# Four more first-use places for expert 0's weights, router logits in four column groups, and transposes by token chunk

## What is computed

```python
def expert_choice_ffn(h, w_router, w_gate, w_up, w_down):
    B, S, D = h.shape                              # 1, 512, 1024
    cap = EC_CAPACITY_FACTOR * S // N_EXPERTS      # 2 * 512 // 16 = 64
    logits = jnp.einsum('bsd,de->bse', h.astype(jnp.float32), w_router.astype(jnp.float32))
    affinity = jax.nn.softmax(logits, axis=-1)
    top_w, top_idx = lax.top_k(affinity.transpose(0, 2, 1), cap)
    xe = jax.vmap(lambda hb, ib: hb[ib])(h, top_idx)
    hid = jax.nn.silu(jnp.einsum('becd,edf->becf', xe, w_gate)) * jnp.einsum('becd,edf->becf', xe, w_up)
    ye = jnp.einsum('becf,efd->becd', hid, w_down) * top_w[..., None].astype(h.dtype)
    combine = lambda yb, ib: jnp.zeros((S, D), h.dtype).at[ib.reshape(-1)].add(yb.reshape(-1, D))
    return jax.vmap(combine)(ye, top_idx)
...
        x = x + gate1 * token_mixer(h, ...)
        h = rms_norm(x, norm_ffn_w[l]) * (1.0 + scale2) + shift2
        x = x + gate2 * expert_choice_ffn(h, ...)
```

## Time and profile before

| | |
|---|---|
| median of three runs | 2085.09 us |
| the profiled execution, its own time | 2085.79 us |
| its span (first to last instruction) | 2084.0 us |
| TensorE busy, matmuls | 1924.8 us, 92% |
| VectorE busy | 684.4 us, 33% |
| ScalarE busy | 463.1 us, 22% |
| DMA bytes | 513.42 MB, mean 246 GB/s |

### The profile page before, as it was taken

The page is one execution under the profiler, slowest core; times in us unless marked ns, Lnnn a source line. Parts: engine busy times, 40 slices in busy tenths (PEclk is TensorE's granted clock), DMA queues, the critical chain, the costliest instruction groups (busy, mean ns, idle before and its releaser), DMA issues.

```text
span 2084.0 us, 20330 instructions
## 1 busy us (share of the span) xinstructions
PE 1924.8 (92%) x8674; PEld 1156.3 (55%) x8674; DVE 684.4 (33%) x943; ACT 463.1 (22%) x685; POOL 32.7 (2%) x41
## 2 busy tenths in 40 slices
PE   5999979999879999889999999898999999999998
PEld 5876766567544434343433434343344478888887
DVE  5474464375321111211110021101038842322334
ACT  5347445212201001010100001010031422222222
POOL 0000000000000000000000000000030000000000
PEclk9999989999989999999999999999999999999999
DMA  7211110484649999999999999999971105323211
GB/s 300 84 51 48 61 41 21 178 300 188 262 195 421 421 421 421 422 421 421 421 422 421 421 421 421 421 421 421 392 234 41 41 23 169 91 91 101 101 61 41
DMA packets 131775, 513.42 MB, mean 246 GB/s; under 512 B 8035, under 2 KB 70627, under 8 KB 81379
## 3 DMA queue, kind: packets, MB, share of 16 engines
q1 hardware_dynamic: 127312, 487.95, 59.2%
q10 hardware_dynamic: 4374, 24.18, 3.0%
HBM read 510.00 MB, written 2.10 MB: 246 GB/s over the span
## 4 chain that ended last, share of the span: by engine, by line
PE 69%; DMA 19%; DVE 7%; ACT 3%; issue 2%; POOL 0%; SPq 0%; ACTq 0%; DVEq 0%; POOLq 0%
DMA work<-in_w_exp_up 11%; PE ps L1119 11%; PE ps L1080 7%; DMA ring<-in_w_exp_up 6%; PE ps L1284 5%; PE ps L534 5%; PE ps L1244 4%; PE ps L1243 4%; PE ps L1245 4%; PE ps L550 3%; PE ps L1007 3%; PE ps L551 3%; PE ps L552 3%; PE ps L733 2%; PE ps L1105 2%
## 5 line engine op out<-in xcount | busy, mean ns | idle before, releaser
L1080 PE MATMUL ps<-work 128*64 128x512 f32 x1208 | 328.8, 594 | 25.7 <-DMA work<-in_w_exp_up 25.7
L1080 PE MATMUL ps<-ring,work 128*64 128x512 f32 x720 | 216.8, 594 | 15.0 <-DMA ring<-in_w_exp_up 15.0
L1080 PEld LDWEIGHTS ps<-work 128*64 128x64 f32 x1208 | 112.0, 137 | 201.2 <-issue 149.5
L2206 DVE TENSOR_TENSOR work<-work,ps 64x512 f32<-64x512 f32 x64 | 42.0, 691 | 477.4 <-ACT work L1650 476.7
L1650 ACT ACTIVATE work<-ps 64x512 f32<-64x512 f32 x64 | 32.6, 584 | 734.4 <-PE ps L1080 734.4
L534 PE MATMUL ps<-work,ring 128*128 128x512 f32 x320 | 138.9, 592 | 0.7 <-issue 0.7
L1119 PE MATMUL ps<-work 128*64 128x512 f32 x568 | 135.1, 628 | 4.2 <-issue 3.6
L1243 PE MATMUL ps<-xh,wh 128*128 128x512 f32 x352 | 137.0, 389 | 0.0
L1245 PE MATMUL ps<-xh,wl 128*128 128x512 f32 x352 | 136.9, 389 | 0.0
L1244 PE MATMUL ps<-xl,wh 128*128 128x512 f32 x352 | 136.9, 389 | 0.0
L2339 DVE TENSOR_TENSOR wl<-ring,wh 128x2048 fp32r<-128x2048 f32 x33 | 75.6, 2292 | 180.2 <-ACT wh L1738 180.2
(11 more groups left out here) (337 smaller groups left out, 2604.4 us busy)
## 6 DMA issues: line engine op xcount, KB each, us to landing
work<-in_w_exp_gate SPq DMA_DIRECT2D x76, 1024.0 KB, 26.7
work<-in_w_exp_up SPq DMA_DIRECT2D x75, 1024.0 KB, 27.3
work<-in_w_exp_down SPq DMA_DIRECT2D x71, 1024.0 KB, 27.0
ring<-in_w_exp_gate SPq DMA_DIRECT2D x45, 1024.0 KB, 26.7
ring<-in_w_exp_up SPq DMA_DIRECT2D x45, 1024.0 KB, 27.0
ring<-in_w_exp_down SPq DMA_DIRECT2D x42, 1024.0 KB, 26.8
ring<-in_w_in SPq DMA_DIRECT2D x27, 1024.0 KB, 6.4
work<-in_ada_w ACTq DMA_DIRECT2D x16, 1024.0 KB, 6.6
```

Source lines behind the costliest of these rows:

```text
L1080: i = e.matmul(PS[64 * gu:64 * gu + 64, fb, :], at(XET + 128 * k + 64 * z, 64), flat(key)[:, 512 * fb:512 * fb + 512], start=(k == 0), sto ...
```

## The change

- **Places.** Four are added: 19, 20 and 21 lie over `YE`, the residual `X` and the first part of `HIDT` (hidden values, transposed), 22 over `SG` (silu's output; until the logits are done the same space holds the first half of `H2T`). `HIDT` and `XET` change their order for it. Each is used once, by expert 0: 21 and 22 by its last gate and up piece (`eg`, `eu` of `k` = 7), 19 and 20 by its 4th and 5th down piece. The first three open when the last chunk of `XS2` is written, the fourth when the logits are done. From the 22nd expert piece on, the cycle of 17 goes on as before, four pieces later.
- **Residual.** Since `X` is overwritten, the first pair's results are added to `XS2` times the root mean square instead (`st2 + 4`), and the sum is written to `X`. For this the reciprocals go to `st2`.
- **Transposes.** All 8 `k` of a token chunk are transposed as soon as the chunk is in `XS2`, each `k` into a bank of its own (`T2_BANKS`).
- **Logits.** They stand behind all transposes; slice `k` goes to the rows from 32 (k mod 4) of bank 2, so that four partial sums arise. DVE copies 128 x 512 instead of 16 x 512, and the turn to tokens x experts is a product with a 128 x 16 matrix of ones and zeros (built by one new small DVE reduction) that also adds the four groups.
- **Gather.** For the first pair, `k` 0 to 4 stand ahead of expert 0's first gate and up slice, `k` 5 to 7 between its first and its second.
- Some semaphores are merged (`ap_vc` into `ap_va`, `a_lb` into `a_c`, `mu_pe` and `vr_pe` into `ln_pe`, `l_gf` into `l_vec`), with the same order.

The core of the diff:

```diff
-SLOT = [HEAD + W * i for i in range(NR0)] + [SG + W * (i + 1) for i in range(3)] + [HT, HT + W] + [HIDT + 1024 + W * i for i in range(5)] + [DEAD]
+SLOT = [HEAD + W * i for i in range(NR0)] + [SG + W * (i + 1) for i in range(3)] + [HT, HT + W] + [XET + 1024 + W * i for i in range(5)] + [DEAD]
 SLOT += [HGT, PT + 3072]
+SLOT += [YE, YE + W, YE + 2 * W, SG]
...
     cycle = (12, 13, 14, 15, 8, 16, 2, 4, 7, 11, 9, 10, 1, 5, 3, 0, 6)
-    slots += [cycle[i % 17] for i in range(len(ex))]
+    slots += list(cycle[:14]) + [21, 22] + list(cycle[14:]) + [19, 20] + [cycle[(i - 4) % 17] for i in range(21, len(ex))]
...
-                    elif slot == 6:
+                    elif slot in (6, 22):
                         e.wait_ge(s["wo_pe"], 8)
                         e.wait_ge(s["rt_pe"], 1)
+                    elif slot in (19, 20, 21):
+
+                        e.wait_ge(*normed(2, 3))
...
                 e.wait_ge(*turned_k(2, k))
-                if k == 0:
-                    e.wait_ge(s["wo_t"], 5)
-                return e.matmul(PS[0:16, 4, :], at(O_VEC + VEC["wr"][0] + 16 * k, 16), at(H2T + 512 * k, 512), start=(k == 0), stop=(k == KD - 1))
+                g = 32 * (k % 4)
+                return e.matmul(PS[g:g + 16, 2, :], at(O_VEC + VEC["wr"][0] + 16 * k, 16), at(H2T + 512 * k, 512), start=(k < 4), stop=(k >= 4))
...
-            turn(XS2, [0, 1, 2, 3], lambda c: normed(2, c), t2_free, s["t_pe"], lambda k: logits(k - 2) if k >= 2 else None)
-            logits(KD - 2)
-            logits(KD - 1).then_inc(s["rt_pe"], 1)
+            for c in range(TC):
+                e.wait_ge(*normed(2, c))
+                for k in range(KD):
+                    if c == 0:
+                        t2_free(k)
+                    i = e.transpose(bank(T2_BANKS[k], 128, 128 * c), at(XS2 + 1024 * c + 128 * k, 128), ident)
+                    if c == TC - 1:
+                        i.then_inc(s["t_pe"], 1)
+            for k in range(KD):
+                i = logits(k)
+            i.then_inc(s["rt_pe"], 1)
+
+            def logits_by_token():
+                for tc in range(TC):
+                    p = e.matmul(bank(5, 16, 16 * tc), at(WKT + 128 * tc, 128), at(rst, 16), start=True, stop=True)
+                p.then_inc(s["rt_pe"], 1)
...
-            gather(0)
+            gather(0, range(5))
             for ex in range(NE):
                 z, p = ex % 2, ex // 2
                 for k in range(KD):
 
+                    if (ex, k) == (0, 1):
+                        gather(0, range(5, KD))
...
+            own(e.tensor_reduce(at(rst, 16), raw(O_CST + CST["ident"][0], [(1, 16), (32, 4)]), AX, ALU.add))
             e.wait_ge(s["rt_pe"], 1)
             e.wait_ge(*rooted(2, 3))
-            e.tensor_copy(rows(0, 16, WKT, 512), PS[0:16, 4, :]).then_inc(s["rt_d"], 1)
+            e.tensor_copy(at(WKT, 512), bank(2)).then_inc(s["rt_d"], 1)
...
+                if p == 0:
+
+                    e.scalar_tensor_tensor(out=xa, in0=at(XS2 + 1024 * tc + 512 * dh, 512), scalar=at(st2 + 4 + tc, 1), in1=bank(6 + dh),
+                                           op0=ALU.mult, op1=ALU.add).then_inc(s["x_ca"], 1)
+                    return
                 e.tensor_tensor(xa, xa, bank(6 + dh), ALU.add).then_inc(s["x_ca"], 1)
```

More of the change, by code:

```diff
@@ L72 @@
 XS2, H2T = PT, HT + 4096
-AFFT, WKT = X + 4096, X + 4608
+AFFT, WKT = X + 5120, X + 5632
 SG = HT + 4096
 YE = X - 1024
-XET, HIDT = X + 4096, X + 5120
+HIDT, XET = X + 4096, X + 5120
 OH, OHW, OHWT = GATE1, GATE1 + 512, O_SMALL + NSMALL - 512
@@ L175 @@
 SEMS = (
-    "l_vec l_cst l_x l_ab l_gf l_out "
-    "own_act own_dve p_zero a_c d_small a_lb d_ada "
+    "l_vec l_cst l_x l_ab l_out "
+    "own_act own_dve p_zero a_c d_small d_ada "
     "r_a r_d sc1 t_pe t_d t_a ac_pe "
@@ L361, in rooms_of @@
             return piece(key, 4 if kind in ("wo", "o2") else 8)
+        T2_BANKS = (2, 3, 4, 5, 6, 7, 0, 1)
         FS_O2, FS0 = 4, 8
@@ L617, in hg_proj @@
                     if g < 2 and pr == 1:
-                        e.wait_ge(*((s["ap_w"], 5), (s["ap_va"], 1))[g])
+                        e.wait_ge(*((s["ap_w"], 5), (s["ap_va"], 2))[g])
                     elif g in (2, 3):
@@ L694, in at_proj @@
                 norm_rot(4)
-                e.wait_ge(s["ap_vc"], 1)
+                e.wait_ge(s["ap_va"], 1)
                 for tc in range(TC):
@@ L822, in values @@
                     if u == 0:
-                        e.wait_ge(s["ap_va"], 1)
+                        e.wait_ge(s["ap_va"], 2)
                     e.wait_ge(s["at_c"], 2 * u + 2)
@@ L974, in _ @@
             e.wait_ge(s["rt_d"], 1)
-            e.wait_ge(s["wo_t"], 6)
-            by_token()
+            logits_by_token()
             e.wait_ge(s["rt_d"], 3)
@@ L994, in hidden, with gather @@
                 return rows(64, 128, SG + 512 * fb + 256 * (q // 2), 256).rearrange("p (i a) -> p i a", a=2)[:, :, q % 2]
-            def gather(p):
-                e.wait_ge(s["x_oh"], p + 1)
-                for k in range(KD):
+            def gather(p, ks=range(KD)):
+                if ks[0] == 0:
+                    e.wait_ge(s["x_oh"], p + 1)
+                for k in ks:
                     if k == 0 and p > 0:
@@ L1070, in _ @@
                     for fb in range(4):
[L1071 to L1075, removed]
+                        if k == 0 and ex > 0:
+                            e.wait_ge(s["x_hd"], 4 * ex - 3 + fb)
                         for gu, kind in ((0, "eg"), (1, "eu")):
@@ L1188, in _ @@
                 p = e.matmul(bank(4), cst("o512"), at(CV + 512 * i, 512), start=(i == 3), stop=(i == 1))
-            p.then_inc(s["mu_pe"], 1)
+            p.then_inc(s["ln_pe"], 1)
             pool_dense(10, 1, 4)
@@ L1196, in _ @@
                 p = e.matmul(bank(5), cst("o512"), at(TP + 512 * i, 512), start=(i == 0), stop=(i == 3))
-            p.then_inc(s["vr_pe"], 1)
+            p.then_inc(s["ln_pe"], 1)
             pool_dense(13, 0, 4)
@@ L1314, in _ @@
             e.wait_ge(s["d_small"], 1)
-            e.activation(at(lbs, 8), at(lbe, 8), ACT.Exp).then_inc(s["a_lb"], 1)
+            e.activation(at(lbs, 8), at(lbe, 8), ACT.Exp).then_inc(s["a_c"], 1)
             def rms(x, scr, st, chunks, ready, done):
@@ L1336, in turned @@
                         ready()
-                    put(k, bank(banks[k % 4])).then_inc(s["t_a"], 1)
+                    put(k, bank(banks[k % len(banks)])).then_inc(s["t_a"], 1)
             def half_hi(n):
@@ L1424, in at_proj @@
                 e.wait_ge(s["ap_q"], 4)
-                e.activation(at(TMP + 1024, 512), bank(1), ACT.Copy).then_inc(s["ap_vc"], 1)
+                e.activation(at(TMP + 1024, 512), bank(1), ACT.Copy).then_inc(s["ap_va"], 1)
                 for n in ahead(half_no[("at", 2), 1]):
@@ L1712, in _ @@
             pool_out(12, 2)
-            e.wait_ge(s["vr_pe"], 1)
+            e.wait_ge(s["ln_pe"], 2)
             e.wait_ge(s["cv_pe"], 1)
@@ L1833, in _ @@
                 ada_step(k, ACC)
-            e.wait_ge(s["a_lb"], 1)
+            e.wait_ge(s["a_c"], 2)
             own(e.reciprocal(at(lbr, 8), at(lbs, 8)))
@@ L1840, in rms @@
             def rms(i, x, xs, st, chunks, ready):
+                inv = st if i == 2 else st + 4
                 for c in chunks:
                     e.wait_ge(*rooted(i, c))
-                    own(e.reciprocal(at(st + 4 + c, 1), at(st + 4 + c, 1)))
+                    own(e.reciprocal(at(inv + c, 1), at(st + 4 + c, 1)))
                     ready(c)
-                    e.tensor_scalar(at(xs + 1024 * c, 1024), at(x + 1024 * c, 1024), at(st + 4 + c, 1), None, ALU.mult).then_inc(s["r_d"], 1)
+                    e.tensor_scalar(at(xs + 1024 * c, 1024), at(x + 1024 * c, 1024), at(inv + c, 1), None, ALU.mult).then_inc(s["r_d"], 1)
             e.wait_ge(*rooted(1, 3))
@@ L1870, in turned @@
                     e.wait_ge(*turns(i, k))
-                    put(k, bank(banks[k % 4])).then_inc(s["t_d"], 1)
+                    put(k, bank(banks[k % len(banks)])).then_inc(s["t_d"], 1)
             for k in range(KD):
@@ L2320, in _ @@
             pool_window(2)
-            e.wait_ge(s["mu_pe"], 1)
+            e.wait_ge(s["ln_pe"], 1)
             e.wait_ge(s["cv_d"], 93)
@@ L2396, in fin_scale @@
                 if tc == 0:
-                    e.wait_ge(s["l_gf"], 16)
+                    e.wait_ge(s["l_vec"], 32)
                 e.wait_ge(s["fin_x"], 2 * tc + 2)
```

16 lines of the change are left out of this document (9 added, 7 removed).

## The result

The changed kernel takes 2067.49 us (median of four runs, 2067.22 to 2070.18) against 2085.74 for the kernel before in the same series (four runs): 0.9918 of the time, 95% interval 0.9906 to 0.9931, 18.25 us less. Two further series gave 17.1 and 16.3 us less (0.9915 and 0.9921). The forecast was 2065.5, with a range of 2061.5 to 2070.5, and 19.6 us less. So the time lies in the range, and the gain was forecast 1 to 3 us too large.

The account below looks back on a forecast made before the run. The prediction took an unbroken stream of expert weight loads to bound the kernel; -10.0 (places) - 10.8 (earlier release) + 1.2 (hole) = -19.6 us gave a median of 2065.5 us, range 2061.5 to 2070.5.

Parts of the forecast that it names:

- The bound: Expert stage: its end is the end of an unbroken load stream at 421 GB/s; all behind follows at fixed distance.
- The four places, -10.0: Early expert loads: four more pieces fit into idle DMA time before the stream restarts, 2.49 us each, -10.0 us.
- Logits, -8.3: Router: transposes per chunk and side-by-side logits let DVE's logits copy start at 557.4 instead of 565.71, -8.3 us.
- Turn to tokens, +0.3: Router, behind the logits: four products with 128 x 128 weights instead of 16 x 128 cost +0.3 us.
- Gather, -2.8: First pair's gather: 24 records moved behind expert 0's first gate and up slice, so that slice starts 2.8 us earlier.
- the release: First two reused places, after expert 0's first gate and up slice: freed at 588.7 instead of 599.5, -10.8 us.
- The hole of +1.2: Stream's restart: next two releases come 6.2 us later, two pieces fill only 4.98, so DMA idles, +1.2 us.
- The 18th piece, 0.6 us to spare: Stream in expert 0's down: piece waits for the sixth down piece at 631.6, needed at 632.2; no loss.
- the second rival: Reuse distance binds: PE late in expert 0, pieces 15 to 20 wait, total 2068 to 2075.5 us; chance 0.08.
- The groups overlap: Against the rival that the logits' column groups run one after another: +4.2 us, total 2069.7; chance 0.12.
- The places are filled in time: Against the rival that the extra places fill too late, nothing new in place at restart: 2075.5 us; chance 0.04.
- The clock rose within the gather as before: Against the rival that the clock stays at 1.2 GHz through expert 0's gate and up: +26, 2092 us; chance 0.02.

Follow-up runs that it names:

- The late doubled gather: Changed kernel with the gather products of the pair of experts 8 and 9 made twice: 2068.25 us, distance to last `eu` landing 934.5 us.

## Why the prediction was right, and where it was off

**The bound.** Right. The end of the expert stage moves with the last `eu` piece (18.5 us) and nothing behind it changes (583.8 and 583.9 us). The late doubled gather costs nothing, at a busy share that looks like a bound.

**The four places, -10.0.** Right: alone -9.9 by the median, and by the distance once the shorter gather is taken out of its -10.4. The two of them that were taken out cost 4.2 us of distance, 5.0 less the 0.8 of the hole that went with them. They are filled by about 576 (forecast 578) and the stream restarts at 590.

**Logits, -8.3.** The copy comes 8.63 us earlier, counted from the last addition. The copies out of PSUM ran four in a row on both engines, a little faster than by the pair that I had (0.74 instead of 0.83 each):

```profile
551.89 2.97 DVE L2161 TENSOR_SCALAR work<-ps,stay 128x512 f32<-128x512 f32 x4 [0.52 <-PE ps L978]
```

```profile
551.90 2.79 ACT L1654 ACTIVATE work<-ps,stay 128x512 f32<-128x512 f32 x4 [1.52 <-PE ps L978]
```

**Turn to tokens, +0.3.** Mis-sized: 1.08 instead of 0.43, +0.65, since the products come as two records each (x8 against x4). That the copy came 0.3 earlier than forecast makes up for this miss, by luck. And I had taken all behind as unchanged, while the next transposes (L999) took 1.04 us at a granted clock of 0.50, before 0.60 us at 1.00. Up to the gather's start the distance shrank by 7.5 us, not 8.0.

**Gather, -2.8.** The 40 records took 7.16 us, of which I had expected 6.8; the first product of expert 0 came 10.0 us earlier from the last addition, not 10.8, and with it the release (41.05 against 51.06). As a term of the sum it is -2.5.

**The hole of +1.2.** Right, 1.2 (291 GB/s in the window). The prediction's 27.67/8 is 3.46, not 3.43, which moves nothing.

**The 18th piece, 0.6 us to spare.** This step failed. I had divided expert 0's down, 15.65 us, evenly by eight. The clock falls at its start, before and after. The trace of the kernel before had it already: its down began at 628.08, and SP issues on the first piece's release 3.32 us later, not 1.96.

```profile
631.40 0.33 SPq L524 DMA_DIRECT2D work<-in_w_exp_up  x1
```

The changed kernel's windows of PE (us, busy, PEclk, DMA share, GB/s):

```profile
618.00:620.00 2.00, 1.50 (x11) 1.00 1.01 422
620.00:622.00 2.00, 1.94 (x6) 0.60 1.01 422
622.00:624.00 2.00, 2.00 (x8) 0.55 1.02 418
624.00:626.00 2.00, 2.00 (x12) 1.00 0.99 406
```

So the first down piece takes about 3.4 us (SP issues on its release at 623.49, the down began at 620.06), the others 1.7 to 1.95, and the first six take 12.2 instead of 11.7:

```profile
623.49 0.33 SPq L530 DMA_DIRECT2D ring<-in_w_exp_up  x1
625.44 0.33 SPq L530 DMA_DIRECT2D ring<-in_w_exp_gate  x1
627.16 0.33 SPq L530 DMA_DIRECT2D work<-in_w_exp_up  x1
632.31 0.33 SPq L530 DMA_DIRECT2D work<-in_w_exp_gate  x1
```

The piece that waits for the sixth is issued at 632.31, when the stream needs it at 588.50 + 1.2 + 17 x 2.49 = 632.0: 0.3 us late instead of 0.6 early. Of these 0.9 us, 0.5 are the uneven down; 0.4 are its start, which comes 31.6 us behind the first release, not 31.2 (my "8.2 earlier" was also 0.2 more than the -8.0 that it stands on). It is the second rival, in a mild form: 0.8 us lost in this execution, 1.0 and 1.0 in the two other traces. That more is lost than the 0.3 of this count stays open. I had given the rival 0.08 for 2.5 us and more.

**The sum by measured terms.** -10.0 (places), -10.0 (release), +1.2, +0.8 to +1.0: -17.9, against a distance of -17.4. The forecast of -19.6 came near the first series (-18.25) because its two misses, 0.8 of release and 1 of reuse, are small; that this series shows a larger gain than the two others (-17.1 and -16.3) is luck, 1.0 us of it in the profiled execution the mixer's.

**The other rivals.** The groups overlap (0.88 against 0.40 us a product). The places are filled in time. The clock rose within the gather as before: 0.72 in the window 580 to 585, 1.00 from 585 on. The tail's loads are issued from 1498.34 on, 26.8 us ahead of PE's first use at 1525.13, before 26.5.

## What to carry to other kernels

Where a stage runs off an unbroken stream of loads, find when the stream starts and how many pieces are in place by then: each piece placed into idle DMA time ahead of it is worth its whole transfer time, and an earlier first release is worth its own length, but both only up to the point where the stream overtakes the readers of the places that it reuses. Work that room out with the real times of the first few readers, not with the average of a group, since a short stretch of half clock fell on just those in every trace here. Once the room is used up, a further step ahead (here the gather's split) is paid back at the next place.

## What the runs showed of the hardware

Loads of 1 MiB ran at 421 GB/s for 850 us without a break, with 27 to 30 us from issue to landing in the full queue. Products into different column groups overlap at 16 columns as at 64: eight logits took 3.20 us in four groups, 7.04 in one. The granted clock fell to half (0.60 and 0.55 in two windows of 2 us) around 620 us, for 3.4 us in all, although PE had run at full rate for 30 us up to 615.6. Between the two lay 16 small transposes, 2.52 us, and 2.0 us of idle time, 1.44 ahead of them for the silu and 0.56 behind:

```profile
616.97 2.52 PE L1125 MATMUL ps<-stay,work 64*128 64x64 f32 x16 [1.44 <-DVE work L2233]
```

Every trace shows the fall at the start of expert 0's down. Expert 1's down took the same 15.65 us in the changed kernel, expert 2's 13.95. I hadn't expected so short a pause to be followed by a fall, and not that it would set the time of the one reader that the stream was waiting for. That the pause causes it was not tried.
